# Joint attention: sigmoids of the gate features by logarithm and exponential on ACT, and three of four query banks turned inside the first iterations

## The reference, cut to what matters

```
aq, ak, av, hu, ag, hg = split(h @ w_in)            # h: 512 rows x 1024
q = rope(rms_norm(aq, 8 heads)); k = rope(rms_norm(ak, 2 heads)); v = av
y_a = softmax attention(q, k, v)                    # 8 query heads on 2 key heads; context rows see context only
y_b = hyena(hu)                                     # short convolution, then two long ones by Fourier products
y   = [y_a * silu(ag), y_b * silu(hg)]              # silu(g) = g * sigmoid(g)
x   = x + gate * (y @ w_out)
```

## Time and profile before

| | |
|---|---|
| Runs | 1548.74, 1549.86, 1550.76 us; median 1549.86 |
| Profiled execution | 1551.57 us, its span 1549.7 us, mean granted PE clock 0.989 |
| PE busy | 1491.2 us, 96% |
| DVE busy | 948.3 us, 61% |
| ACT busy | 784.8 us, 51% |
| Joint attention in the trace | 1040.6 (first turned head) to 1187.0 us (last values) |

### The profile page before, as it was taken

The page is one execution under the profiler, slowest core; times in us unless marked ns, Lnnn a source line. Parts: engine busy times, 40 slices in busy tenths (PEclk is TensorE's granted clock), DMA queues, the critical chain, the costliest instruction groups (busy, mean ns, idle before and its releaser), DMA issues.

```text
span 1549.7 us, 21508 instructions
## 1 busy us (share of the span) xinstructions
PE 1491.2 (96%) x8288; PEld 1197.9 (77%) x8288; DVE 948.3 (61%) x1703; ACT 784.8 (51%) x1333; POOL 91.3 (6%) x142
## 2 busy tenths in 40 slices
PE   7999999999999999998999999999999999999897
PEld 6887777799887787877789978787776448788776
DVE  4554456766555554455857665676579874669664
ACT  5445785455434454787345544444443302343773
POOL 6050000000000000000000000000000000042120
PEclk9999999999999999999999999999999999999999
DMA  8782434787554854242689655363122001164200
GB/s 277 247 184 82 134 112 163 217 238 218 197 187 142 303 183 136 85 133 82 206 245 244 190 187 167 135 163 82 55 82 69 27 1 38 46 183 136 70 28 28
DMA packets 183413, 220.96 MB, mean 143 GB/s; under 512 B 6587, under 2 KB 103397, under 8 KB 183312
## 3 DMA queue, kind: packets, MB, share of 16 engines
q1 hardware_dynamic: 179088, 211.65, 43.5%
q0 software_dynamic: 3184, 7.93, 2.5%
q10 hardware_dynamic: 1040, 0.00, 0.0%
HBM read 216.55 MB, written 3.01 MB: 142 GB/s over the span
## 4 chain that ended last, share of the span: by engine, by line
PE 73%; DVE 16%; ACT 7%; issue 3%; DMA 1%; DVEq 0%; SPq 0%; ACTq 0%
PE bank L618 20%; PE bank L619 19%; PE bank L620 19%; DVE w_low L1778 3%; ACT w_high L1344 2%; DVE arena L2181 2%; PE bank L858 1%; PE bank L1093 1%; PE bank L699 1%; PE bank L802 1%; PE bank L1056 1%; PE bank L833 1%; PE bank L635 1%; DMA raw<-in_w_up 1%; PE bank L1069 1%
## 5 line engine op out<-in xcount | busy, mean ns | idle before, releaser
L1778 DVE TENSOR_TENSOR w_low<-raw,w_high 128x1024 fp32r<-128x1024 f32 x344 | 415.2, 1213 | 341.0 <-ACT w_high L1344 335.8
L1344 ACT ACTIVATE w_high<-raw 128x1024 fp32r<-128x1024 f32 x352 | 367.0, 1047 | 339.1 <-PE bank L620 288.0
L618 PE MATMUL bank<-w_high,acts_r 128*128 128x512 f32 (+1 forms) x848 | 340.0, 401 | 11.7 <-DVE w_low L1778 5.0
L619 PE MATMUL bank<-w_low,acts_r 128*128 128x512 f32 (+1 forms) x848 | 330.5, 390 | 0.0
L620 PE MATMUL bank<-w_high,acts_r 128*128 128x512 f32 (+1 forms) x848 | 330.4, 390 | 0.0
L618 PE MATMUL bank<-acts_r,w_high 128*128 128x256 f32 (+1 forms) x736 | 229.2, 311 | 2.5 <-DVE arena L2199 2.4
L619 PE MATMUL bank<-acts_r,w_high 128*128 128x256 f32 (+1 forms) x736 | 226.0, 307 | 0.0
L620 PE MATMUL bank<-acts_r,w_low 128*128 128x256 f32 (+1 forms) x736 | 225.9, 307 | 0.0
L618 PEld LDWEIGHTS bank<-w_high,acts_r 128*128 128x128 f32 x848 | 160.8, 190 | 53.8 <-DVE w_low L1778 6.6
L620 PEld LDWEIGHTS bank<-w_high,acts_r 128*128 128x128 f32 x848 | 159.8, 188 | 36.7
L619 PEld LDWEIGHTS bank<-w_low,acts_r 128*128 128x128 f32 x848 | 160.4, 189 | 32.1
(11 more groups left out here) (317 smaller groups left out, 1812.1 us busy)
## 6 DMA issues: line engine op xcount, KB each, us to landing
raw<-in_w_in SPq DMA_DIRECT2D x69, 1024.0 KB, 5.3
raw<-in_w_up SPq DMA_DIRECT2D x64, 512.0 KB, 6.6
raw<-in_w_down SPq DMA_DIRECT2D x32, 1024.0 KB, 5.0
raw<-in_w_ada SPq DMA_DIRECT2D x24, 1024.0 KB, 6.9
raw<-in_w_in SPq DMA_DIRECT2D x34, 512.0 KB, 5.2
raw<-in_w_o SPq DMA_DIRECT2D x8, 1024.0 KB, 6.9
raw<-in_w_out SPq DMA_DIRECT2D x8, 1024.0 KB, 5.0
raw<-in_w_out_c SPq DMA_DIRECT2D x4, 768.0 KB, 5.3
```

The lines of the kernel that those rows point to most:

```text
L618: mm(o, lh, rh, start=start, stop=False)
L619: mm(o, lh, rl, start=False, stop=False)
L1344: run(A_(high, src, ACT.Copy), (high_ready, n + 1))
L1778: run(V.tensor_tensor(low, src, high.bitcast(F32), ALU.subtract), split_done(n))
```

## The change

It has two parts. **Sigmoids:** in the joint attention ACT follows exp(-g) by ln(1+x) and exp(-x), as in the second layer; DVE's addition and reciprocal go, and only the multiplication by g stays. **Heads:** ahead of the attention only the two key banks and query bank 0 are turned. Query banks 1, 2 and 3 are turned in iterations 1, 2 and 3, behind the turned probabilities and ahead of the filler, on banks 5 to 7; DVE takes their low parts in its next iteration, behind the inverted sums. DVE's features of groups 1 and 2 move from ahead of the attention into its iteration 0, behind the maxima of pair 0. The second layer's attention keeps its order.

```diff
-        late_heads = {i: (group,) for i, group in enumerate(((2, 0), (2, 1), (3, 0), (3, 1), (3, 2), (3, 3)))}
+        late_heads = ({1: (0, 1), 2: (0, 2), 3: (0, 3)},
+                      dict(enumerate(((2, 0), (2, 1), (3, 0), (3, 1), (3, 2), (3, 3)))))
...
-                    o = open_bank("heads", l, j, b, among=ANY_BANK if only is None else GATE_BANKS[2:])
+                    o = open_bank("heads", l, j, b, among=among)
...
+            def turn_joint_heads(j, b, among):
+
+                if j == 0:
+                    turn_heads(0, 0, lambda c, t: q2[:, t, c * P:(c + 1) * P], 4, T4, 1, b, among)
                 else:
-                    turn_heads(1, 3, lambda c, t: nk[:, t, c * P:(c + 1) * P], 4, T4, 1, b)
+                    turn_heads(0, 1, lambda c, t: k2d[:, t, c, :], KVH, T4, 1, b, among)
+
+            def turn_late_heads(l, j, b):
+
+                if l == 0:
+                    turn_joint_heads(j, b, GATE_BANKS)
...
                         second(2 * i - 1)
-                    if l == 1 and i in late_heads:
-                        for group in late_heads[i]:
-                            turn_late_heads(*group)
+                    if i in late_heads[l]:
+                        turn_late_heads(l, *late_heads[l][i])
                     advance(filler, per_pair if i < PAIRS else 1000)
...
-            turn_heads(0, 1, lambda c, t: k2d[:, t, c, :], KVH, T4, 1)
-            turn_heads(0, 0, lambda c, t: q2[:, t, c * P:(c + 1) * P], 4, T4, 1)
+            for j, b in ((1, 0), (1, 1), (0, 0)):
+                turn_joint_heads(j, b, ANY_BANK)
             attention2(0, filler, 8)
...
                     act.wait_ge(*filled(*key))
-                    run(A_(dst[c // 4][:, c % 4, :], bank(*key)[:, 0:n], ACT.Exp, scale=-1.0), silu_exp.by(l, c) if l == 0 else None)
-
-            def take_sigmoid(key):
+                    run(A_(dst[c // 4][:, c % 4, :], bank(*key)[:, 0:n], ACT.Exp, scale=-1.0))
+                    if l == 0:
+                        take_sigmoid(0, key)
+
+            def take_sigmoid(l, key):
 
                 c = key[2] - HY_CH
-                g = (wgT, ngT)[c // 4][:, c % 4, :]
+                g = ((ag, hg), (wgT, ngT))[l][c // 4][:, c % 4, :]
                 run.settle()
                 run(A_(g, g, ACT.Ln, bias=eps_col[:, 1:2]))
                 run.settle()
-                run(A_(g, g, ACT.Exp, scale=-1.0), silu_exp.by(1, c))
+                run(A_(g, g, ACT.Exp, scale=-1.0), silu_exp.by(l, c))
...
-            for j, n in ((1, KVH), (0, QH // 2)):
-                for b in range(n):
-                    act.wait_ge(*filled("heads", 0, j, b))
-                    take_high(A_((qT2, kT2)[j][:, 0, b, :], bank("heads", 0, j, b)[:, :], ACT.Copy), "heads", 0, j, b)
+            for j, b in ((1, 0), (1, 1), (0, 0)):
+                take_head_high(0, j, b, due=False)
             attention2(0)
...
                 dve.wait_ge(*silu_exp.at(l, c))
-                if l == 0:
-                    run(V.tensor_scalar(g, g, 1.0, None, ALU.add))
-                    run.settle()
-                    run(V.reciprocal(g, g))
-                    run.settle()
                 run(V.tensor_tensor(g, g, bank(*key)[:, 0:n], ALU.mult), emptied(*key))
...
                     if l == 0:
-                        for key in ended_in[(2, i - 1)] if i else ():
+                        for key in ended_in[(2, i - 1)] if i else ended_in[(2, "before")][1:]:
                             take_features(0, key)
...
                         invert_sums(i - 1)
-                    if l == 1 and i - 1 in late_heads:
-                        for group in late_heads[i - 1]:
-                            take_head_low(*group)
+                    if i - 1 in late_heads[l]:
+                        take_head_low(l, *late_heads[l][i - 1])
...
-            take_heads_low((1, 0), (0, 0))
-            take_features(0, before[0])
-            take_heads_low((1, 1), (0, 1))
-            take_features(0, before[1])
-            take_heads_low((0, 2))
-            take_features(0, before[2])
-            take_heads_low((0, 3))
+            for j, b in ((1, 0), (0, 0), (1, 1)):
+                take_head_low(0, j, b)
+            take_features(0, ended_in[(2, "before")][0])
             attention2(0)
```

More of the change, by code:

```diff
@@ L1012, in feature_groups, with turn_heads @@
                         yield
-            def turn_heads(l, j, src, chunks, tiles, per_bank, only=None):
+            def turn_heads(l, j, src, chunks, tiles, per_bank, only=None, among=ANY_BANK):
                 pe.wait_ge(*heads_ready.at(l, j))
                 for b in range(chunks // per_bank) if only is None else (only,):
-                    o = open_bank("heads", l, j, b, among=ANY_BANK if only is None else GATE_BANKS[2:])
+                    o = open_bank("heads", l, j, b, among=among)
                     for m in range(per_bank):
@@ L1021, in turn_heads @@
                     close_bank(ins, "heads", l, j, b)
-            def turn_late_heads(j, b):
-                if j == 2:
-                    turn_heads(1, 2, lambda c, t: nq[:, t, c * P:(c + 1) * P], 4, TILES, 2, b)
-                else:
-                    turn_heads(1, 3, lambda c, t: nk[:, t, c * P:(c + 1) * P], 4, T4, 1, b)
+            def turn_joint_heads(j, b, among):
+                if j == 0:
+                    turn_heads(0, 0, lambda c, t: q2[:, t, c * P:(c + 1) * P], 4, T4, 1, b, among)
+                else:
+                    turn_heads(0, 1, lambda c, t: k2d[:, t, c, :], KVH, T4, 1, b, among)
+            def turn_late_heads(l, j, b):
+                if l == 0:
+                    turn_joint_heads(j, b, GATE_BANKS)
+                elif j == 2:
+                    turn_heads(1, 2, lambda c, t: nq[:, t, c * P:(c + 1) * P], 4, TILES, 2, b, GATE_BANKS[2:])
+                else:
+                    turn_heads(1, 3, lambda c, t: nk[:, t, c * P:(c + 1) * P], 4, T4, 1, b, GATE_BANKS[2:])
             def attention2(l, filler, per_pair):
@@ L1586, in take_sigmoid, with take_head_high @@
                 run.settle()
-                run(A_(g, g, ACT.Exp, scale=-1.0), silu_exp.by(1, c))
-            def take_head_high(j, b, due=True):
-                key = ("heads", 1, j, b)
+                run(A_(g, g, ACT.Exp, scale=-1.0), silu_exp.by(l, c))
+            def take_head_high(l, j, b, due=True):
+                key = ("heads", l, j, b)
                 if due:
@@ L1594, in take_head_high @@
                 act.wait_ge(*filled(*key))
+                if l == 0:
+                    take_high(A_((qT2, kT2)[j][:, 0, b, :], bank(*key)[:, :], ACT.Copy), *key)
+                    return
                 x = (wqT, wkT, nqT, nkT)[j][0]
@@ L1631, in attention2 @@
                         splits.due("s", 2 + l, 2 * i + 1)
-                    if l == 1 and i in late_heads:
-                        for group in late_heads[i]:
-                            take_head_high(*group, due=False)
+                    if i in late_heads[l]:
+                        take_head_high(l, *late_heads[l][i], due=False)
                     for key in ended_in[(3, i - 1)] if l and i else ():
-                        take_sigmoid(key)
+                        take_sigmoid(1, key)
                     for key in ended_in[(2 + l, i)]:
@@ L1728, in _ @@
             for b in range(KVH):
-                take_head_high(1, b)
+                take_head_high(1, 1, b)
             heads_rsqrt(1, 2, TILES * QH)
             for b in range(2):
-                take_head_high(0, b)
+                take_head_high(1, 0, b)
             for t in range(T4):
@@ L2200, in take_features, with take_head_low @@
                                                in1=u[:, s, 0:SEQ - 1], op0=ALU.mult, op1=ALU.add), emptied(*key) if s else None)
-            def take_head_low(j, b):
-                key = ("heads", 1, j, b)
+            def take_head_low(l, j, b):
+                key = ("heads", l, j, b)
                 dve.wait_ge(*high_done[key])
+                if l == 0:
+                    x = (qT2, kT2)[j]
+                    run(V.tensor_tensor(x[:, 1, b, :], bank(*key)[:, :], x[:, 0, b, :].bitcast(F32), ALU.subtract), emptied(*key))
+                    return
                 high, low = (wqT, wkT, nqT, nkT)[j]
@@ L2472, in _ @@
             for b in range(KVH):
-                take_head_low(1, b)
+                take_head_low(1, 1, b)
             heads_norm(1, 2, nq, TILES, QH, 4, False, None, [("in2", 1, 2, t) for t in range(TILES)], after_nq[0:2])
             for b in range(2):
-                take_head_low(0, b)
+                take_head_low(1, 0, b)
             dve.wait_ge(bias_loaded, BIASES * 16)
```

## The result

The changed kernel takes 1541.53 us (median of 4 runs, 1540.76 to 1542.78) against 1550.31 of the kernel before (4 runs beside it, 1548.74 to 1551.59). The ratio is 0.9942 with a 95% interval of 0.9930 to 0.9955. The profiled execution took 1540.82 us, its span 1539.0 us at a mean granted clock of 0.997.

A forecast was written before the change was run, and what follows sets the result against it. PE was taken to bound nearly all the joint attention, with gains only at its two ends: start 3.1 plus end 3.7 gave 6.8 us, so 1549.86 - 6.8 = 1543.0 us, range 1539.0 to 1547.2.

The forecast's parts named there:

- The start: Start of the joint attention: moving twelve transposes gains 4.26 us, less 1.15 for the clock, giving 3.1 us.
- 4.26 us if the clock holds: Attention start: pair 1's scores come 5.70 us earlier, less 1.44 us for twelve transposes in pairs 1 to 3.
- 1.15 us of clock: Attention start, group 3: half of the 2.29 us that the slow clock cost there before, taken as loss.
- two splits of 1.22: DVE after 1046.0: two weight splits of 1.22 us counted ahead of groups 1 and 2's convolutions.
- hidden with 0.5 us to spare: Before group 4: DVE frees group 2's bank at 1053.6 us, and PE wants it at 1054.1.
- 1189.26 instead of 1195.29: Behind the last gate group: DVE's taps begin at 1189.26 us, so the second spectra come 6.03 us earlier.
- Six of these are worth nothing by themselves: Inside the attention: six of eight gate groups' 0.42 + 3.35 us on DVE gain nothing, as PE never waited.
- The clock at the end: Before the second spectra: PE's 3.1 us wait may slow the clock; 2.29 us taken off 6.03, leaving 3.7.
- The clock staying up at both places: Rival: no clock fall at the attention's start or before the second spectra, 1539.6 us; chance 0.12.
- the end wins nothing: Rival: another engine is just behind DVE after the attention, so only the start's 3.1 us remain, 1546.8 us; chance 0.13.
- The gate banks' mechanism: Slower rival, pairs 1 to 3: PE waits for DVE to empty banks 5 to 7, up to 17.3 us, 1560.3; chance 0.05.
- the one ACT_TABLE_LOAD: ACT's trace: one table load of 1.28 us at 1.23 us, read as showing logarithm and exponential change no table.

The follow-up runs named there:

- experiment 3: The changed kernel with only the last two gate groups' sigmoids on ACT, the first six with addition and reciprocal on DVE: 1541.49 us, ratio 0.9944.
- experiment 4: The changed kernel with two more ACT copies of g onto itself between logarithm and exponential of each of the eight gate groups: 1545.83 us, ratio 0.9959.
- experiment 12: A second run of the changed kernel with two extra ACT copies of g in each of the eight gate groups: 1544.39 us, ratio 0.9965.
- experiment 1: The changed kernel with addition and reciprocal of all eight gate groups back on DVE, only the turned heads moved: 1545.85 us, ratio 0.9970.
- experiment 2: The kernel before with only the sigmoids moved to ACT, the heads as they were: 1544.98 us, ratio 0.9963.
- experiment 10: The changed kernel with the second key bank's low part behind group 0's convolution, and groups 1 and 2 ahead of DVE's iteration-0 splits: 1541.72 us.
- Experiment 6: The changed kernel with DVE's low part of the second key bank behind group 0's convolution instead of ahead of it: 1541.28 us, ratio 0.9943.
- experiment 11: The changed kernel with 3.8 us of extra DVE work in iteration 0, ahead of the splits and groups 1 and 2's convolutions: 1549.09 us, ratio 0.9989.
- experiment 8: The changed kernel with addition and reciprocal of the last two gate groups on DVE again, the first six on ACT: 1544.46 us, ratio 0.9963.
- experiment 5: The changed kernel with DVE's product of attention output and gate moved behind the second taps' mixing (values differ): 1539.63 us, ratio 0.9930.
- experiment 9: The changed kernel with the attention's gate product on POOL, second key bank's low part later, groups 1 and 2 ahead of iteration-0 splits: 1539.03 us.

## Why the prediction was right

The forecast was 1543.0 us (1539.0 to 1547.2) and a gain of 6.8; measured were 1541.5 and 8.8. Of these 2.0 us of gain 0.45 are the kernel before, whose median was 1549.86 in the runs that the forecast started from and 1550.31 beside the changed kernel. Most of the rest is the clock, which was costed too high.

**What bounds the kernel** was read rightly: in the pairs nothing counted of ACT's or DVE's sigmoids (experiments 3, 4 and 12), and the two ends were independent (experiments 1 and 2).

**The start**: 3.1 us forecast, 2.86 in the profile. The step "4.26 us if the clock holds" measured 3.97, and "1.15 us of clock" measured 1.11 in the changed kernel's profile and nothing in the others. That the 1.15 came so close is luck: it was a mean of nothing and 2.29, while the profiles show nothing, 1.56, 1.96 (experiment 2) and 2.29 us lost in group 3, and the 1.11 is 1.56 less a wait that was not forecast (below). In one of eight profiles with the same waits before the scores and group 3 the clock fell, so the term is near 3.8. What was off by 0.3 us is in the step that gave DVE "two splits of 1.22" before group 2's bank is free. DVE's rows of the changed kernel have three:

```profile
1045.80 3.49 DVE L1789 TENSOR_TENSOR w_low<-raw,w_high 128x1024 fp32r<-128x1024 f32 x3
```

So "hidden with 0.5 us to spare" was wrong: the cover was gone whenever the clock held, by some 0.4 us (142.45 - 141.48 of experiment 10, less the 0.6 won before group 3). PE's rows of the head and group 4 show it, first in experiment 1, then in the changed kernel's profile:

```profile
1052.05 0.60 PE L1021 MATMUL bank<-ident,arena 128*128 128x128 f32 x4
1052.79 0.50 PE L619 MATMUL bank<-acts_r,w_high 128*128 128x512 f32 x1
```

```profile
1053.53 0.60 PE L1021 MATMUL bank<-ident,arena 128*128 128x128 f32 x4
1053.88 0.48 PE L619 MATMUL bank<-acts_r,w_high 128*128 128x512 f32 x1
```

From the head to the group it is 0.74 us and 0.35. In the changed kernel's profile the slow group 3, 1.56 us longer than 5.77, hid the wait, so only 1.11 of the 1.56 lengthened the start. Experiment 6 shows it as a wait, 10 removes it, and 11 prices it at one for one, plus clock.

**The sigmoids**: "1189.26 instead of 1195.29", 6.03 us, measured 6.13 (ACT 0.60, 0.72 and 0.63 us for the forecast 0.60, 0.75 and 0.66). "Six of these are worth nothing by themselves" holds once the last two are moved; experiment 8 adds that they carried a backlog of 3.7 us as long as the last two stayed on DVE, which the prediction did not say. "PE never waited for them" was no proof of that: the backlog was DVE's, and PE paid for it behind the attention.

**The clock at the end** is the term that was mis-sized: 2.29 us were taken. It measured nothing in the changed kernel's profile, and 1.4 to 1.7 in six of seven profiles with that wait, 1.4 on average. The prediction had taken the 2.29 us over from the start; no run shows them at this place. With the 1.4, end 4.7 and start 3.8 sum to 8.5 us, against 8.8 measured. PE's wait itself was forecast at 3.1 and measured 3.13.

**The rivals.** The clock staying up at both places came true in experiment 1's start and the changed kernel's end, but in no profile at both. That the end wins nothing is refuted by the end itself, 27.90 us instead of 34.03, with DVE's chain busy 24.55 of 25.60 us in both profiles. No other engine is just behind it: experiment 5 takes another 2.20 us off the end. The gate banks' mechanism exists and its margin was thinner than stated. The page of the Trainium skill that was weighed against the change (ScalarE: Activation LUTs, What ACT_TABLE_LOAD costs) prices a switch to another set of functions. No switch takes place here: ACT's logarithm starts 0.62 us behind the first exponential, which takes 0.60, and the second exponential 0.76 us behind the logarithm, which takes 0.72.

The prediction read "the one ACT_TABLE_LOAD" wrongly. The trace of the kernel before has three of 1.28 us each, at 1.2, 905.8 and 921.0 us, and the changed kernel's has them at 1.2, 904.2 and 919.4. The argument holds all the same, since both traces have none behind these, and the gates' logarithms come later (from 1126.4 us in the changed kernel's).

## What to carry to other kernels

Where one engine is busy without a gap for a whole stage, look for the time at the stage's two ends: here the backlog of the others, and the order in which they empty the banks, were paid there. Removing the last instances of a slow instruction from such a queue can be worth all of the gain, and the earlier ones only what backlog they leave. Count what a moved piece of work falls behind, weight splits that happen to be due included, before calling it hidden; and price each wait of PE at its length plus a chance of a slow clock for the next group.

## What was not expected of the hardware

A product over SBUF of 128x2048 float32 took DVE 2.28 us alone and 3.41 us when it began 1.26 us before the end of POOL's product of the same size (4.54 us). So DVE lost 1.13 of the 1.26 us that the two ran beside each other, nearly all, and not a share of the whole product. Three of DVE's products with one operand in PSUM (128x512, 0.62 to 0.68 us) lie inside POOL's span and were not slowed at all. This is one profile (experiment 9).

The same wait of 3.1 us before the same work was followed by a clock fall in six profiles and by none in one. At the start a wait of 1.7 and one of 1.3 us, with 1 us of work between, were followed by a fall during group 3 in one profile of eight. In the kernel before and in experiment 2, with waits of 2.5 and 2.3 us in the same place, it fell both times.
